# One transformer layer with a 32-expert mixture: routing tail, first gather, load sizes of the second and third expert pair, and the seams of the last two pairs rearranged

## What is computed

```
ht = rms_norm(x, g_ffn)
logits = (ht @ w_router + b_router)
top_val, top_idx = lax.top_k(logits, TOP_K)          # 4 of 32
gates = jax.nn.softmax(top_val, axis=-1)
# for each expert e, on the tokens that chose it:
hu = xb @ w_up[e] + b_up[e]                          # 1024 -> 2 x 1024
x_glu, x_lin = jnp.split(hu, 2, axis=-1)
act = min(x_glu,7) * sigmoid(1.702 * min(x_glu,7)) * (clip(x_lin,-7,7) + 1.0)
y = act @ w_down[e] + b_down[e]                      # 1024 -> 1024
x = x + sum over its experts of y * gate
```

## Time and profile before

| | |
|---|---|
| median of 3 runs | 1029.41 us |
| the profiled execution, its time | 1030.23 us |
| its span (first to last instruction) | 1028.2 us |
| TensorE busy, of the span | 982.9 us, 96% |
| DMA queue of the weights, share of 16 engines | 97.2% |
| bytes moved | 425.06 MB, mean 413 GB/s |
| granted TensorE clock, mean | 0.985 |

### The profile page before, as it was taken

One profiled execution on the slowest core, in us unless ns is written; L12 is line 12 of the kernel. 1 busy time (PEld: TensorE's weight loads), 2 busy tenths in 40 slices (PEclk: granted clock), 3 DMA queues, 4 the chain that ended last, 5 costly groups with the idle time before them and its releaser, 6 DMA issues.

```text
span 1028.2 us, 10912 instructions
## 1 busy us (share of the span) xinstructions
PE 982.9 (96%) x4512; PEld 395.4 (38%) x4512; DVE 202.6 (20%) x486; ACT 115.6 (11%) x246; POOL 12.8 (1%) x26
## 2 busy tenths in 40 slices
PE   9999999999999999799898989999898999999998
PEld 5446553434343434243332424343242434332432
DVE  0456132121212121211121111111121121211112
ACT  2427101010101010000000000000000010100000
POOL 0200000000000000000000000000000000000000
PEclk9999999999999999999998999999999999999999
DMA  9985899999999999999999999999999999999996
GB/s 361 413 369 218 324 348 428 422 434 432 422 438 440 433 431 439 433 431 441 431 431 431 434 420 429 426 437 439 428 436 418 435 431 432 428 433 426 429 424 281
DMA packets 22472, 425.06 MB, mean 413 GB/s; under 512 B 3856, under 2 KB 4624, under 8 KB 7472
## 3 DMA queue, kind: packets, MB, share of 16 engines
q1 hardware_dynamic: 22064, 424.17, 97.2%
q10 hardware_dynamic: 384, 0.54, 0.2%
HBM read 423.65 MB, written 1.05 MB: 413 GB/s over the span
## 4 chain that ended last, share of the span: by engine, by line
PE 58%; DMA 40%; SPq 1%; DVE 0%; issue 0%; ACT 0%; POOLq 0%; POOL 0%; DVEq 0%
DMA everything<-in_w_moe 39%; PE psum L1595 20%; PE psum L1543 17%; PE psum L1175 4%; PE psum L1439 4%; PE psum L1308 3%; PE psum L1137 2%; PE psum L1400 2%; PE psum L1150 1%; PE psum L1167 1%; SPq L561 1%; PE psum L1390 1%; PE psum L1492 1%; PE psum L1158 1%; DMA everything<-in_x_turned 0%; PE psum L1448 0%
## 5 line engine op out<-in xcount | busy, mean ns | idle before, releaser
L1543 PE MATMUL psum<-everything 128*64 128x512 f32 x2040 | 448.4, 596 | 6.8 <-DMA everything<-in_w_moe 6.6
L1543 PEld LDWEIGHTS psum<-everything 128*64 128x64 f32 x2040 | 143.3, 137 | 296.3 <-issue 281.7
L1595 PE MATMUL psum<-everything 128*64 128x512 f32 x960 | 226.8, 621 | 31.8 <-DMA everything<-in_w_moe 31.8
L1595 PEld LDWEIGHTS psum<-everything 128*64 128x64 f32 x960 | 69.9, 142 | 174.6 <-issue 171.8
L1102 DVE TENSOR_SCALAR everything<-psum 128x512 f32<-128x512 f32 x32 | 22.1, 692 | 389.4 <-PE psum L1543 389.4
L817 DVE TENSOR_TENSOR everything<-psum,everything 128x512 f32<-128x512 f32 (+1 forms) x38 | 25.0, 663 | 325.9 <-PE psum L1400 310.4
L1439 PE MATMUL psum<-everything 128*128 128x512 f32 x126 | 61.0, 605 | 0.0
L1400 PEld LDWEIGHTS psum<-everything 128*128 128x128 f32 x480 | 54.7, 192 | 12.2 <-issue 12.2
L769 ACT ACTIVATE everything<-everything 128x512 f32<-128x512 f32 x32 | 20.2, 631 | 346.3 <-DVE everything L1102 346.3
L1400 PE MATMUL psum<-everything 128*128 128x128 f32 x480 | 57.6, 278 | 0.0
L1175 PE MATMUL psum<-everything 128*128 128x512 f32 x96 | 42.1, 594 | 0.0
(11 more groups left out here) (168 smaller groups left out, 334.3 us busy)
## 6 DMA issues: line engine op xcount, KB each, us to landing
everything<-in_w_moe SPq DMA_DIRECT2D x22, 4096.0 KB, 38.5
everything<-in_w_moe SPq DMA_DIRECT2D x38, 2048.0 KB, 17.4
everything<-in_w_moe SPq DMA_DIRECT2D x24, 1024.0 KB, 9.4
everything<-in_w_in SPq DMA_DIRECT2D x3, 2048.0 KB, 24.3
everything<-in_w_out SPq DMA_DIRECT2D x2, 2048.0 KB, 11.3
everything<-in_w_moe SPq DMA_DIRECT2D x8, 512.0 KB, 5.8
everything<-in_w_mem_kv SPq DMA_DIRECT2D x1, 2048.0 KB, 16.9
everything<-in_w_in SPq DMA_DIRECT2D x1, 1024.0 KB, 8.6
```

The source lines that it names most:

```text
L1543: mm = pe.matmul(psum[r:r + SLOTS, bank], XT[:, k, r:r + SLOTS], weights[i][:, column:column + N], start=first and k == 0 and j >= half, s ...
L1595: mm = pe.matmul(psum[r:r + SLOTS, DOWN_BANKS[n]], actT[:, 2 * i + k, r:r + SLOTS], slot[:, column:column + N], start=i == 0 and k == 0, s ...
```

## The change

Six groups of edits.

1. **Routing tail.** The squares are scaled in ScalarE and, for the last quarter of x, taken in two halves as VectorE delivers them; GpSimd adds the parts before the root. `choose` loses a memset (done once, ahead) and gains a small product `rs_chosen`. `sel` is made straight from the counts in PSUM; `spots` comes after it. The count of t = 1 does its `ones` matmul before it waits for the choice. The counts get banks of their own (`COUNT_BANKS`).
2. **First gather.** It makes block 0, then blocks 2 and 3 before the up matmuls begin; block 1 is made in the middle of chunk 1, and the count of all tokens (`count_all`) in the middle of chunk 4 instead of ahead of chunk 0.
3. **Loads.** Only chunk 0 (quarters) and chunk 1 (halves) of the second pair come in pieces; chunks 4, 5, 2, 3 of it and chunk 0 of the third pair come whole. SyncE issues 15 loads there instead of 21.
4. **Start of a pair.** The bias of banks 0 and 2 comes before the wait for `xt_ready`. In the second pair only half of the gather comes ahead of chunk 0; the rest, `combine` and the other two biases come before chunk 2.
5. **Last two pairs.** Pair 14 gathers for pair 15 during its down projection (two halves, before chunks 9 and 10) and leaves all four quarters of its `combine` to pair 15, which does them before chunk 2.
6. **Pair 14's loads.** Chunks 8 and 9 come singly instead of as one two.

The diff, cut (allocations, semaphore declarations and bank lists are left out):

```diff
-    SECOND_PIECES = {0: (0, 1, 2), **{j: (0, 2, 4) for j in range(1, 6)}}
-    THIRD_PIECES = (0, 1, 2, 4)
+    SECOND_PIECES = {0: (0, 1, 2), 1: (0, 2, 4)}
...
-                for c0, c1 in zip(THIRD_PIECES, THIRD_PIECES[1:]):
-                    if c1 < 4:
-                        halves += 1
-                        sp.wait_ge(half_used, halves)
-                    else:
-                        wait_used(2, 0)
-                    part = slice(c0 * SLOT_COLS // 4, c1 * SLOT_COLS // 4)
-                    sp.dma_start(slots[0][:, part], chunk(2 * PAIR_CHUNKS)[:, part]).then_inc(two_in[0], 16)
...
-                for d in range(1, TWOS - 1):
+                for d in range(1, TWOS - 2):
...
-                for j, done in ((PAIR_CHUNKS - 2, two_in[TWOS - 1]), (PAIR_CHUNKS - 1, quarters_in[0])):
+                for j, done in zip(range(UP_CHUNKS, PAIR_CHUNKS), (two_in[4], odd_in[4], two_in[5], quarters_in[0])):
...
-            pair(2, 2, single=3, begun=(1, 0, 0))
+            pair(2, 2, single=3)
...
+                last = 2 + t
+                if t == 1:
+                    pool.wait_ge(squares["ffn"], 4)
+                    step(nc.gpsimd.tensor_tensor(ss_half[:, 1:2], ss_half[:, 1:2], ss_half[:, 3:4], ALU.add))
+                    last = 4
+                pool.wait_ge(squares["ffn"], last + 1)
+                step(nc.gpsimd.tensor_tensor(ss_half[:, t:t + 1], ss_half[:, t:t + 1], ss_half[:, last:last + 1], ALU.add))
...
+                parts = ((0, N // 2, x2_half, 1), (N // 2, N, x2_ready, 4)) if c == 3 else ((0, N, x2_ready, c + 1),)
...
-                step(V.memset(top_v[:, t, TOP_K:], GONE))
...
+                dve.wait_ge(chosen_ready, t + 1)
+                step(V.tensor_scalar(rs_chosen[:, t], chosen[:, t, 0:2], rs_ffn[:, t:t + 1], None, ALU.mult))
...
                 dve.wait_ge(placed, t + 1)
+                for e in range(2):
+                    last = V.tensor_scalar(sel[:, t, e * SLOTS:(e + 1) * SLOTS], constant("iota"),
+                                           psum[:, COUNT_BANKS[t], 64 + e:65 + e], rs_chosen[:, t, e:e + 1],
+                                           ALU.is_equal, ALU.mult)
+                last.then_inc((sel_first, sel_ready)[t], 1)
...
+                if t == 1:
+                    pe.matmul(here, ones, chosen[:, 0], start=True, stop=False)
                 pe.wait_ge(chosen_ready, t + 1)
-                mm = pe.matmul(here, before, chosen[:, t], start=True, stop=t == 0)
-                if t == 1:
-                    mm = pe.matmul(here, ones, chosen[:, 0], start=False, stop=True)
-                mm.then_inc(placed, 1)
+                pe.matmul(here, before, chosen[:, t], start=t == 0, stop=True).then_inc(placed, 1)
...
             bias(0, (0, 2), start=True)
-            gather_first(1, range(KD // 2))
-            pe.matmul(psum[:, 4, 256:256 + E], ones, chosen[:, 0], start=True, stop=False)
-            pe.matmul(psum[:, 4, 256:256 + E], ones, chosen[:, 1], start=False, stop=True).then_inc(counted, 1)
+            for ks, done in zip(FIRST_ROWS, (gathered_part, gathered_part)):
+                gather_first(1, ks, done)
...
-                    pe.wait_ge(up_read, 2 * q)
-                    gather(q)
+                    at_once = not second and not last_one
+                    if not last_one:
+                        pe.wait_ge(up_read, 2 * q)
+                        gather(q, range(KD if at_once else KD // 2))
                     pe.wait_ge(y_ready, 2 * q)
-                    if not own:
-                        combine(q - 1, (2, 3), start=second)
-                    pe.wait_ge(xt_ready, 2 * q + 2)
+                    if at_once and not own:
+                        combine(q - 1, (2, 3))
                     pe.wait_ge(whose_ready, q + 1)
-                    bias(p, range(4), start=True).then_inc(biased, 1)
+                    bias(p, (0, 2), start=True)
+                    pe.wait_ge(xt_ready, 2 * q + (2 if at_once else 1))
+                    if at_once:
+                        bias(p, (1, 3), start=True).then_inc(biased, 1)
                 for place, j in enumerate(order):
+                    if j == 2 and (second or last_one):
+                        if second:
+                            gather(q, range(KD // 2, KD))
+                        combine(q - 1, (2, 3) if second else range(4), start=second)
+                        pe.wait_ge(xt_ready, 2 * q + 2)
+                        bias(p, (1, 3), start=True).then_inc(biased, 1)
...
                         if first and i == 0 and j == half + 1:
+                            pe.wait_ge(count_ready, 1)
                             gather_first(0, range(KD // 2, KD))
-                            gather_first(1, range(KD // 2, KD))
+                            gather_first(1, range(KD // 2, KD), gathered)
+                        elif first and i == 0 and j == 1:
+                            gather_first(0, (1,))
+                            gather_first(1, (1,), gathered)
+                        elif first and i == 0 and j == half:
+                            count_all()
...
+                    if next_too and i == 1:
+                        pe.wait_ge(up_read, 2 * q + 2)
+                        gather(q + 1, range(KD // 2))
+                    elif next_too and i == 2:
+                        gather(q + 1, range(KD // 2, KD))
...
-                            if last and (n, k) == (1, 1):
+                            if last and (n, k) == (1, 1) and not next_too:
...
-            with pe.Fori(BDOWN_PAIR + 1, PAIRS - 1) as q:
+            with pe.Fori(BDOWN_PAIR + 1, PAIRS - 2) as q:
                 pair(q, q)
+            pair(PAIRS - 2, PAIRS - 2, next_too=True)
             pair(PAIRS - 1, PAIRS - 1, last_one=True)
```

More of the change, by code:

```diff
@@ L293, in layer_kernel @@
         posf = cols(TILES)
-        top_v = cols(16).rearrange("p (t j) -> p t j", t=TILES)
+        top_v = cols(32).rearrange("p (t j) -> p t j", t=TILES)
         top_neg, top_sum, top_inv = cols(TILES), cols(TILES), cols(TILES)
         top_g = cols(8).rearrange("p (t j) -> p t j", t=TILES)
+        rs_chosen = cols(2 * TILES).rearrange("p (t e) -> p t e", t=TILES)
         count_f = cols(1)
@@ L499, in second_pair, with pair @@
                     credit(d)
-                for c0, c1 in zip(THIRD_PIECES, THIRD_PIECES[1:]):
-                    if c1 < 4:
-                        halves += 1
-                        sp.wait_ge(half_used, halves)
-                    else:
-                        wait_used(2, 0)
-                    part = slice(c0 * SLOT_COLS // 4, c1 * SLOT_COLS // 4)
-                    sp.dma_start(slots[0][:, part], chunk(2 * PAIR_CHUNKS)[:, part]).then_inc(two_in[0], 16)
-            def pair(q, p, single=0, begun=(0, 0, 0)):
+            def pair(q, p, single=0):
                 for d in range(TWOS):
@@ L512, in pair @@
                         for i, done in enumerate((two_in[d], odd_in[d])):
-                            if i >= begun[d]:
-                                wait_used(q, 2 * d + i)
-                                sp.dma_start(slots[2 * d + i], chunk(q * PAIR_CHUNKS + 2 * d + i)).then_inc(done, 16)
+                            wait_used(q, 2 * d + i)
+                            sp.dma_start(slots[2 * d + i], chunk(q * PAIR_CHUNKS + 2 * d + i)).then_inc(done, 16)
                     else:
@@ L1029, in place_and_select @@
                 dve.wait_ge(placed, t + 1)
-                step(V.scalar_tensor_tensor(out=spots[:, t], in0=psum[:, ROUTE_BANKS[t], 64:64 + E], scalar=1.0,
-                                            in1=chosen[:, t], op0=ALU.add, op1=ALU.mult))
[L1032 to L1037, removed]
+                for e in range(2):
[3 more added lines that the diff above has]
+                last.then_inc((sel_first, sel_ready)[t], 1)
+                step(V.scalar_tensor_tensor(out=spots[:, t], in0=psum[:, COUNT_BANKS[t], 64:64 + E], scalar=1.0,
+                                            in1=chosen[:, t], op0=ALU.add, op1=ALU.mult))
+            V.memset(top_v[:, :, 8:8 + TOP_K], GONE)
             build_whose(0)
@@ L1081, in _ @@
             weigh(1)
-            dve.wait_ge(gathered, 1)
-            turned_gain(XT[:, 0:2], psum[:, 6, 0:2 * P], 2 * KD, 0, 2, P).then_inc(xt_first, 1)
-            turned_gain(XT[:, 2:4], psum[:, 6, 2 * P:4 * P], 2 * KD, 2, 2, P).then_inc(xt_ready, 1)
+            for i, (ks, done) in enumerate(zip((*FIRST_ROWS, (1,)), (xt_first, xt_ready, xt_first))):
+                dve.wait_ge(gathered if i == 2 else gathered_part, 1 if i == 2 else i + 1)
+                k, kn = ks[0], len(ks)
+                turned_gain(XT[:, k:k + kn], psum[:, FIRST_GATHER_BANKS[k], k * P:(k + kn) * P], 2 * KD, k, kn, P
+                            ).then_inc(done, 1)
             dve.wait_ge(counted, 1)
@@ L1403, in gather, with gather_first @@
                         mm.then_inc(gathered, 1)
-            def gather_first(t, ks):
```

(32 more changed lines are left out.)

39 lines of the change are left out of this document (20 added, 19 removed).

## The result

The changed kernel takes 1031.29 us (median of 10 runs, 1030.09 to 1032.25) against 1028.86 us of the kernel before in the same call (10 runs). The ratio is 1.0020 with a 95% interval of 1.0012 to 1.0029: slower by 2.4 us. The forecast was 1028.2 us, which is 1.2 us under the median from which the prediction started (1029.41) and 0.7 us under this one; the result lies outside the range (1026.2 to 1031.0). The profiled execution of the changed kernel took 1030.68 us with a span of 1028.8 us.

A forecast was written before the change was run, and what follows sets the result against it. The weight queue was taken to set the end. Lead -1.2, whole chunks +0.7 and third pair's chunk 0 -0.7 gave -1.2 us: profiled 1029.0, median 1028.2 us, range 1026.2 to 1031.0.

The forecast's parts named there:

- What bounds the kernel: Whole kernel: the weight queue's last bytes set the end; 2 to 3 us leaked between 140 and 207 us.
- Whole chunks in the second pair: Second pair's loads: chunks 4 and 5 sent later leave the queue short; 0.7 us lost, of 0 to 1.7.
- the landings: View by when loads land (issue plus time to landing); for whole chunks in the second pair it gave no loss.
- the insertions: Second pair's load time: block 1 and the count of all tokens inside chunks 1 and 4, 0.28 + 0.27 us given back.
- The lead: First pair's start: up matmuls begin 1.2 us earlier, so the first load behind chunk 0 leaves earlier; 1.2 us won, of 0 to 1.3.
- The wash rival: Early start buys nothing, thin supply at chunks 4 and 5 eats the third pair's gain: 0.0 +-0.5 us, chance 0.2.
- the holes: Second pair: times the queue lacks bytes, up to 1.0 us at chunk 4 and up to 0.7 at chunk 5.
- Third pair's chunk 0: Third pair's first load, whole and issued near 193 us: 0.7 us won, of 0 to 1.5.
- Last two pairs, ordinary starts, pair 14's loads: Pair starts, pair 14's single loads, pairs 14 and 15: worth 0; a new 0.7 us TensorE wait is covered.
- The slower rival: Last pair: new wait near 969 us makes TensorE's matmuls slow and late; middle +1.7 us, 1031.1 us, chance 0.13.

The follow-up runs named there:

- whole_only: The kernel before with only chunks 2, 3, 4 and 5 of the second pair loaded whole instead of in halves: 1.7 us slower (1.0018), repeated 1.9 us slower (1.0017).

## Why the prediction was wrong

- *What bounds the kernel:* right. The queue sets the end, bytes not moved between 140 and 205 us are never made good, and the rate from 260 to 940 us is 432 GB/s in every kernel.
- *Whole chunks in the second pair:* the step that failed first, since it alone makes the change slower. I took 0.7 us of 0 to 1.7, "nearer the landings". Measured 1.7 and 1.9 us, at my upper bound and a little over. Three things were wrong in it. The issue of chunk 4 was put at 146.9 us and was 148.0; 0.65 us of that are the insertions, which cost 1.2 and not 0.55 us. Chunk 3, released only by the matmul after it, made a hole of its own, 320 GB/s in 164 to 168 us of whole_only, where I wrote that chunks 2, 3 and 6 come in time. And the lower bound came from a 1 MiB load onto a nearly idle queue (2.9 us above its bytes): chunk 4 took 9.7 us to land, not 7.8, and landed at 157.7 us, later than before and not 1.6 us earlier.
- *The lead:* taken as 1.2 us won of 0 to 1.3, measured 0.0, as large a miss. It was priced at the first load alone, where the bytes did flow earlier (277 GB/s where 143 stood), although the prediction itself left only 0.65 us of it from chunk 4 on; with the insertions at 1.2 us nothing was left. The wash rival had the result of this half right but not the reason: it said that the slowest engine was never without work, and a start 4.3 us later, which cost 4.2, shows no such cover. It also went wrong in letting the third pair pay for the holes.
- *Third pair's chunk 0:* taken as 0.7 us won. Whole at its old time it is worth 0.0. The earlier issue was tested only together with the starts and the last pairs, and nothing showed there either. It left at 194.7 us, not 193.2, and landed at 207.0, not by 206.
- *Last two pairs, ordinary starts, pair 14's loads:* 0, and 0 within the measurement. TensorE waited 0.76 us for ScalarE, where I had 0.7. The slower rival (slow matmuls after the wait) did not occur.
- *Put together:* 1.8 + 0 + 0 + 0 gives +1.8 us, within the interval of the result (+1.2 to +3.0). The three misses are 1.1, 1.2 and 0.7 us. All three terms leaned to the side of gain, and for each the other end of its own range was what came. So the mechanism of each was written down, and the choice within the range failed three times.

## What to carry to other kernels

When a load queue sets the end, the time after its first full moment is what counts, and the piece size at that moment must follow the release: a whole chunk released at its end feeds the queue later than two halves do, and what is lost there is kept to the end. Price such an edit by asking, for every load, whether the one before lasts until the next is released, the last chunk of a group (released by its successor) too. An earlier start is worth something only if it reaches the later loads: follow it through every piece of work inserted behind it, and price what is left. A deliberate delay shows cheaply what the start is worth, but read from the trace how long the delay really was.

## What the runs showed of the hardware

The DMA share hides a thin supply. It stood at 0.92 to 1.03 in windows that moved 320 to 373 GB/s where 431 is usual, at 0.85 with 304 GB/s, and fell far only when little moved (0.64 at 143 GB/s). GB/s is the column to read. And how bytes were cut earlier can matter more than how many are asked for: one more chunk whole instead of in halves, at about 144 us, saved 1.5 us beside whole_only and nothing on the changed kernel. The reason is open.
